# A decoder layer on one core: the triangular inverses of the RWKV part by substitution on VectorE, MoBA heads in pairs, and new orders on four engines

## What is computed

```python
def step(S, inp):                       # RWKV-7, per head (8 heads of 64), over 256 tokens
    r_t, w_t, k_t, v_t, kk_t, a_t = inp
    sa = jnp.einsum('bhvk,bhk->bhv', S, -kk_t)
    S = S * w_t[:, :, None, :] + sa[..., None] * (kk_t * a_t)[:, :, None, :] + v_t[..., None] * k_t[:, :, None, :]
    return S, jnp.einsum('bhvk,bhk->bhv', S, r_t)
...
u = rms_norm(h, norm_mix[l])
z = u @ w_in[l]                         # 1024 x 3328
y_rwkv = rwkv7_time_mix(z[..., :RWKV_IN], ...)
y_moba = moba_attention(q, k, v)        # 8 heads of 64; block 256 = SEQ: plain causal attention here
h = h + jnp.concatenate([y_rwkv, y_moba], axis=-1) @ w_mix_out[l]
h = h + memory_cross_attention(rms_norm(h, norm_xattn[l]), rms_norm(mem, norm_mem[l]), w_xq[l], w_xkv[l], w_xo[l])
a = jnp.square(jax.nn.relu(rms_norm(h, norm_ffn[l]) @ w_ff1[l]))
h = h + a @ w_ff2[l]
out = rms_norm(h, norm_final)
```

## Time and profile before

| | us |
|---|---|
| median of three runs (535.70 to 542.41) | 540.17 |
| the profiled execution, its own time | 539.28 |
| its span, first to last instruction | 537.5 |
| TensorE matmuls busy | 501.6 |
| VectorE busy | 319.7 |
| ScalarE busy | 244.2 |
| GpSimd busy | 34.4 |
| mean granted clock of TensorE | 0.957 |

### The profile page before, as it was taken

How to read it: one execution, slowest core, us unless ns; L and a number is a source line. 1 busy time by engine, 2 the same in 40 slices (tenths; PEclk the granted TensorE clock), 3 DMA queues, 4 the chain that set the end, 5 groups by cost and what they waited for, 6 DMA issues and landing times. The chain is left out here.

```text
span 537.5 us, 13383 instructions
## 1 busy us (share of the span) xinstructions
PE 501.6 (93%) x5926; PEld 464.3 (86%) x5926; DVE 319.7 (59%) x456; ACT 244.2 (45%) x372; POOL 34.4 (6%) x54
## 2 busy tenths in 40 slices
PE   4999999967689799999999999899999999999995
PEld 3999999966568699999999989799899898998984
DVE  4687778874034346467787546837565565655556
ACT  6594763412134242153354436335354453545443
POOL 8200000000000000000430003300000000000000
PEclk9998999997679799999999999989999999999999
DMA  8924547240000033124645323635556555574522
GB/s 256 311 85 154 166 153 233 79 159 5 4 5 4 4 100 111 50 87 149 196 126 172 137 79 95 219 83 195 194 165 224 160 197 195 164 264 157 163 77 78
DMA packets 61421, 73.25 MB, mean 136 GB/s; under 512 B 1314, under 2 KB 51572, under 8 KB 61364
## 3 DMA queue, kind: packets, MB, share of 16 engines
q1 hardware_dynamic: 61284, 72.14, 42.0%
q0 software_dynamic: 80, 0.26, 0.2%
HBM read 71.35 MB, written 1.05 MB: 135 GB/s over the span
## 5 line engine op out<-in xcount | busy, mean ns | idle before, releaser
L1083 ACT ACTIVATE w_hi<-raw 128x1024 fp32r<-128x1024 f32 x130 | 137.2, 1059 | 174.2 <-PE bank L481 110.5
L1593 DVE TENSOR_TENSOR w_lo<-raw,w_hi 128x1024 fp32r<-128x1024 f32 x130 | 160.6, 1240 | 86.9 <-ACT w_hi L1083 86.5
L479 PE MATMUL bank<-op_hi,w_hi 128*128 128x256 f32 x672 | 196.4, 292 | 1.5 <-DVE op_lo L1956 0.7
L480 PE MATMUL bank<-op_lo,w_hi 128*128 128x256 f32 x672 | 192.3, 286 | 0.0
L481 PE MATMUL bank<-op_hi,w_lo 128*128 128x256 f32 x672 | 192.2, 286 | 0.0
L479 PEld LDWEIGHTS bank<-op_hi,w_hi 128*128 128x128 f32 x672 | 131.4, 196 | 3.5 <-DVE op_lo L1956 0.9
L480 PEld LDWEIGHTS bank<-op_lo,w_hi 128*128 128x128 f32 x672 | 131.3, 195 | 0.5
L481 PEld LDWEIGHTS bank<-op_hi,w_lo 128*128 128x128 f32 x672 | 131.1, 195 | 0.0
L496 PE MATMUL bank<-w_hi,op_hi 128*128 128x512 f32 x128 | 50.2, 392 | 0.0
L497 PE MATMUL bank<-w_lo,op_hi 128*128 128x512 f32 x128 | 49.9, 390 | 0.0
L498 PE MATMUL bank<-w_hi,op_lo 128*128 128x512 f32 x128 | 49.8, 389 | 0.0
(11 more groups left out here) (237 smaller groups left out, 590.2 us busy)
## 6 DMA issues: line engine op xcount, KB each, us to landing
raw<-in_w_ff SPq DMA_DIRECT2D x32, 1024.0 KB, 5.3
raw<-in_w_in SPq DMA_DIRECT2D x12, 1024.0 KB, 5.4
raw<-in_w_xkv SPq DMA_DIRECT2D x8, 1024.0 KB, 5.4
raw<-in_w_mix_out SPq DMA_DIRECT2D x4, 1024.0 KB, 4.9
raw<-in_w_xq SPq DMA_DIRECT2D x4, 1024.0 KB, 5.1
raw<-in_w_xo SPq DMA_DIRECT2D x4, 1024.0 KB, 4.9
xval<-in_x SPq DMA_DIRECT2D x2, 512.0 KB, 4.8
raw<-in_w_in SPq DMA_DIRECT2D x2, 512.0 KB, 5.8
```

Source lines behind the costliest of these rows:

```text
L479: mm(dst, wh[:, k, :], op_hi[which][:, k, :], start=first, stop=False)
L480: mm(dst, wh[:, k, :], op_lo[which][:, k, :], start=False, stop=False)
L1083: op(view(w_hi), r, ACT.Copy).then_inc(hi_done, 1)
L1593: tt(view(w_lo), r, view(w_hi).bitcast(f32), ALU.subtract).then_inc(lo_done, 1)
```

## The change

It does four things.

1. The transposed matrices (`nmat`) and the eight products by powers go. VectorE inverts the diagonal blocks of 16 itself (`blocks`): it transposes squares of 32x32 so that each partition holds one block, runs a forward substitution of 14 steps of two instructions over all 128 lanes at once, and transposes back, once straight and once turned.
2. Two products on TensorE (`join`) make the inverse of the whole 32x32 matrix from the diagonal blocks and the corner, and one `solve` applies it. `carry` and `solved` go.
3. MoBA heads run in pairs: the two heads of a pair take the two row halves of the array for the scores and the two column halves for the values, in alternating instructions, and share their ScalarE and VectorE steps where shapes allow.
4. The lists of TensorE, ScalarE and VectorE stand in a new order. `mem` is loaded late; `mats` comes after 42 quarters instead of 55; `residual` and other pieces move; one more quarter stands ahead of `rms(3)`.

```diff
-            def product(b, lhs, rhs):
-                for u in range(NU):
-                    for c in range(4):
-                        last = mm(B[b][chunk(c), CH * u:CH * u + CH], powers[lhs][chunk(c), u, :],
-                                  powers[rhs][chunk(c), u, :], start=True, stop=True)
-                return last
...
+            def join(step):
+                pe.wait_ge(dve_blocks, 1)
...
+                for u in range(NU):
+                    n, h = divmod(u, NH)
+                    corner = X[:, 2 * n + h % 2, 128 * (h // 2):128 * (h // 2) + CH]
+                    for c in range(4):
+                        lhs, rhs = (corner, powers[3][:, u, :]) if step == 0 else (powers[2][:, u, :], powers[4][:, u, :])
+                        last = mm(B[step][chunk(c), CH * u:CH * u + CH], lhs[chunk(c)], rhs[chunk(c)], start=True, stop=True)
+                last.then_inc(pe_join, 1)
...
+            def blocks():
+                dve.wait_ge(dve_mats, 2)
+                dve.wait_ge(dve_side, 1)
+                squares = lambda x: x.rearrange("p u (b t) -> p t b u", b=2)
+                link(nc.vector.transpose(turned.rearrange("p t (b u) -> p t b u", b=2), squares(powers[0])))
+                link(tt(low, turned[:, :, 0:BLK], turned[:, :, BLK:2 * BLK], ALU.add))
+                for t in range(1, BLK - 1):
+                    step = rank_one[:, 0:(BLK - 1 - t) * t].rearrange("p (a j) -> p a j", j=t)
+                    shape = [128, BLK - 1 - t, t]
+                    below = low[:, t + 1:BLK, 0:t]
+                    link(tt(step, low[:, t + 1:BLK, t:t + 1].to_broadcast(shape), low[:, t:t + 1, 0:t].to_broadcast(shape), ALU.mult))
+                    link(tt(below, below, step, ALU.add))
+                link(nc.vector.memset(flat(low)[:, 0:BLK * BLK:BLK + 1], 1.0))
+                for b in range(2):
+                    last = ts(wide[0][:, :, BLK * b:BLK * b + BLK], low.rearrange("p t j -> p j t"), side[:, b:b + 1], None, ALU.mult)
+                link(last)
+                nc.vector.transpose(squares(powers[3]), wide[0].rearrange("p t (b u) -> p t b u", b=2)).then_inc(dve_blocks, 1)
...
+            def pair_scores(i):
...
+                for n, e in ((n, e) for n in range(NT) for e in range(2)):
+                    r, keys = slice(HD * e, HD * e + HD), 128 * (n + 1)
+                    last = mm(B[4 + e][:, 128 * n:128 * n + keys], mqk[r, i, tokens_of(n)], mqk[r, 4 + i, 0:keys],
+                              start=True, stop=True)
...
+            def pair_values(i):
...
+                for e in range(2):
+                    mm(B[5][HD * e:HD * e + HD, 0:256], mval[:, 0, cols(2 * i + e)], probT[:, e, 0:256], start=True, stop=False)
```

More of the change, by code:

```diff
@@ new lines, in values @@
+            def values(h):
+                pe.wait_ge(act_turn, h + 1)
+                pe.wait_ge(dve_scores, min(h + 2, XH))
+                if h:
+                    pe.wait_ge(dve_values, h)
+                pe.wait_ge(out_taken, KIND["xv"][h] + 1)
+                for a in range(2):
+                    for k in range(2):
+                        c = XD * h + 128 * a
+                        last = mm(B[4][:, 256 * a:256 * a + 256], xval[:, k, c:c + 128], xprobT[:, k, :],
+                                  start=(k == 0), stop=(k == 1))
@@ L940, in _ @@
             bonus()
[L941 removed]
+            dense(1)
             mats(0)
             mats(1)
[L944 to L959 removed]
+            spread(1)
@@ L960, in _ @@
+            right(0)
+            right(1)
+            load(1, 0)
+            load(1, 1)
+            dense(1)
             right(2)
-            eighth(1)
+            dense(1)
             right(3)
-            values("m", 2)
-            inverse()
-            turn("m", 3)
-            scores("m", 4)
+            dense(4)
+            join(0)
+            dense(1)
+            join(1)
+            load(1, 2)
+            load(1, 3)
+            dense(6)
+            pair_scores(0)
             solve(0)
@@ L1354, in _ @@
             hi(19)
             hi(20)
-            factor()
             hi(21)
+            tokens()
             hi(22)
+            vtokens()
             hi(23)
+            right(0)
+            load(1, 0)
+            load(1, 1)
+            right(1)
+            right(2)
+            right(3)
             hi(24)
-            scores("m", 0)
             hi(25)
+            join()
             hi(26)
+            load(1, 2)
+            load(1, 3)
             hi(27)
             hi(28)
-            turn("m", 0)
@@ L1385, in _ @@
[L1385 to L1404 removed]
+            hi(31)
@@ L1941, in weigh, with pair_scores @@
-            def weigh(who, h):
-                dve.wait_ge(act_prob, head_no(who, h) + 1)
+            def pair_scores(i):
+                dve.wait_ge(pe_pair, i + 1)
+                if i:
+                    dve.wait_ge(pe_flip, i)
+                for e in range(2):
+                    last = stt(out=prob[:, e, :], in0=B[4 + e][:, 0:384], scalar=HD ** -0.5, in1=causal[:, :],
+                               op0=ALU.mult, op1=ALU.add)
+                link(last)
+                for n in range(NT):
+                    last = nc.vector.reduce_max(small[:, 2 * n:2 * n + 2], prob[:, :, 128 * n:128 * n + 128 * (n + 1)], AX.X, negate=True)
+                last.then_inc(dve_pair, 1)
@@ L2035, in _ @@
             lo(18)
-            keys(1)
+            keys(3)
             take(8)
@@ L2056, in _ @@
             tokens()
-            scores("m", 1)
+            take(9)
+            lo(21)
+            bonus()
+            bonus_bias()
+            lo(22)
+            lo(23)
+            diagonal_of(1)
+            mats(0)
+            spread_copy(1)
+            mats(1)
+            sides()
+            blocks()
+            lo(24)
+            take(10)
+            take(11)
+            lo(25)
+            load(1, 0)
+            load(1, 1)
+            inverse()
+            load(1, 2)
+            load(1, 3)
@@ L2058, in _ @@
+            lo(26)
+            take(12)
             lo(27)
-            weigh("m", 1)
             lo(28)
-            bonus()
             lo(29)
-            bonus_bias()
-            mats(0)
-            mats(1)
-            nmat(0)
-            nmat(1)
-            take(12)
+            pair_scores(0)
+            solve(2)
+            pair_weigh(0)
             take(13)
+            solve(3)
             lo(30)
-            values("m", 0)
-            square()
-            scores("m", 2)
@@ L2154, in _ @@
             operand("mix", 2)
+            take(23)
+            lo(50)
             take(24)
```

870 lines of the change are left out of this document (355 added, 515 removed).

## The result

The changed kernel took 501.8 us in the median of four executions (505.9, 497.7, 496.3 and one of 1568.8 us, whose cause is not known), the kernel before 538.3 us beside it. The forecast was 503: close to the median, and some 7 us above these three. But for the one of 1568.8, executions of the changed kernel lie further apart than those of before (494 to 507 us against 536 to 542), and the first profile was taken of a long one, 505.9 us; a second one, taken later of the same kernel, is of a short one, 496.1 us.

The account below looks back on a forecast made before the run. TensorE was taken as the bound, its middle stretch as the place to gain. 539.3 - 17.7 - 17.2 - 3.0 - 4 - 1.6 - 1.4 - 2 + 2 + 2 + 6 = 502.4, predicted as 503 us, range 489 to 516.

Parts of the forecast that it names:

- Small matmuls and stops: TensorE's middle stretch: 1,152 small records removed, -17.7 us; fewer stops at blocks of 256 instructions, -17.2 us.
- 30.4 us of stops before: Middle stretch, kernel before: sixteen blocks with 32.0 us of work wait 16 x 3.9 - 32.0 = 30.4 us.
- floor of 3.9 us per block: A block of 256 TensorE instructions takes at least about 3.9 us; seven short blocks then wait 13.2 us after.
- the cut into single blocks: TensorE's instruction list of each kernel, cut into blocks of 256 with each record's own pace, to count the stops.
- Would-show list: Signs if right: 38 packets, stops only around `mats`, joins, `outq`, 3.5 to 4.3 us apart, `gate` near 211 us.
- Blocks on VectorE: `blocks` ahead of the first join: 10.6 us in all, 11.4 to be covered by 14.6 on TensorE, so 0.
- waits of +2 behind it: +1 us for splits and takes waiting behind `blocks`, +1 for `outq`, whose last copy stands behind a weigh.
- +2 of the early stretch: Up to about 78 us: VectorE prepares the earlier `mats` at nine tenths busy; +2 us of waits, most at `keys`.
- Pairs: MoBA heads run two together in different array halves: -4 us, between 0 and -6.6.
- Start: First dense quarter runs ahead of the parameters, whose DMA cost 1.63 us: -1.6 us.
- `rms(3)`: One more quarter ahead of `rms(3)`, where TensorE waited 2.45 us for GpSimd: -1.4 us.
- +6 for two dips: Dense quarters behind `mats` and `outq` run at halved clock, two dips of 3.0 us each: +6 us.

Follow-up runs that it names:

- burst: The changed kernel plus 368 unused small products in one piece, ten dense quarters behind `rms(3)`: 524.6 us, ratio 0.965 to the kernel before.
- same_half: The changed kernel with both heads of a MoBA pair on the same half of the array: 510.6 us, ratio 0.947 to the kernel before.
- spread: The changed kernel plus 368 unused small products, eight behind each of 46 dense quarters after `rms(3)`: 523.0 us, ratio 0.970 to the kernel before.
- chunks: The changed kernel plus 368 unused small products in eight pieces of 46, five dense quarters between pieces: 508.7 us, ratio 0.946 to the kernel before.
- late_blocks_2: The changed kernel with eight more chained copies of 512 elements inside `blocks` on VectorE: 501.3 us, ratio 0.931 to the kernel before.

## Why the prediction was right, step by step

**Small matmuls and stops.** The mechanism held: 128 matmuls per stop, no semaphore, 38 packets, and -12 us when six products are taken from the kernel before. The sizes were less good. The 30.4 us of stops before are not idle time that the trace shows: from `mats` to `phi` TensorE was idle for 16.9 us, in nine stops and not sixteen, and the other 16.5 us stand in its busy time (60.8 less 44.3 of own work), at a mean clock of 0.78. The size of what remains was taken as 13.2 us from a floor of 3.9 us per block, read in a stretch where the DMA engines stood idle (0.08). There the period was right: 3.5 to 3.7 us in `burst`. In the new places weights are being loaded, and from stop to stop it was 5.9 us (89.52 to 95.44) and 6.0 (115.61 to 121.63). Against that, the cut into single blocks had a stop at every crossing, and `burst` ran 247 records before its first one, so it passed one crossing without a stop. The errors have opposite signs: 8.5 us in the short execution, 15.7 in the long one. Behind `gate`, where dense work is long, the view of waits has no stop without a semaphore in either profile of the changed kernel (from 206.93 and 216.90 to the end); among small matmuls and just behind them (L443) it has, and 368 small ones in one piece cost about 12 us more than in eight, the clock included (20.5 less 8.7).

**Would-show list.** "Each ending 3.5 to 4.3 us after the last one" failed for the reason just given. "Only around `mats`, the joins and `outq`" failed by the stop at L443, which begins 1.5 us behind the joins. The idle time ahead of `rms(3)` was 0.45 us where about 1.0 was forecast. `gate` at 206.9 or 216.9 lies on either side of 211.

**Blocks on VectorE.** Its timeline (of the first profile):

```profile
99.43 1.06 DVE L1740 STREAM_TRANSPOSE neu<-neu 128x512 f32<-128x512 f32 x1
...
100.98 0.17 DVE L1746 TENSOR_TENSOR neu<-neu 128x14 f32<-128x14 f32 x1
...
108.59 1.13 DVE L1752 STREAM_TRANSPOSE neu<-neu 128x512 f32<-128x512 f32 x1
```

The 28 steps, the first of them shown, last from 100.98 to 107.6, 6.6 us where 6.4 were estimated. The three transposes are 1.06, 1.13 and 1.17 us and not 0.69: the whole is 11.9 us, not 10.6. The cover held as worked out, since even twice 0.69 left room; the first join at 111.61 comes 1.9 us behind the signal. So this term stayed 0, and the waits of +2 behind it came to 0.3 (L442 above). The +2 of the early stretch are about right: 0.6 us at 18.6, 0.8 at 65.9, 0.2 at `keys`.

**Pairs.** -4 was too small: -6.6, the bound, is what the rows show (8 records in 0.86 and 0.80 us, where one head took 0.85 and 0.8), and `same_half` takes 5.1 of it away. A pair takes what one head took before (0.86 against 0.85 us for the scores); on the same half it takes 1.50.

**Start.** -1.6 for the earlier first quarter was wrong: 0. The step that failed is that the forecast priced the removed wait at the front and didn't ask what the later row sums make late behind it. The forecast nowhere had the slow pace of the start (dense matmuls 0.21 us apart in the kernel before from 12.15 to 16.0, though the granted clock is 1.00 there), which ended at 12.5 and 13.3 us instead of 17 in the two profiles of the changed kernel, and early with the old order of the start too (its first dense matmuls 0.12 us apart stand at 13.91).

**`rms(3)`.** -1.4 was too small: the wait is 2.0 us shorter, and the forecast left out the halved clock behind it. At 0.21 us instead of 0.12, the 23 dense matmuls from 349.5 to 354.2 had cost 2.2 us more. In all 3.8 us are saved behind `gate`.

**Clock.** The forecast's 0.12 and 0.21 us per dense matmul, and with them its quarter of 1.44, are the pace of the earlier trace rows: 20.30 to 20.42 at a granted clock of 1.00 (20.2 to 22.0), and 0.21 to 0.22 at 0.50 (45.08 to 45.30, 349.51 to 349.72). +6 for two dips was too much for the dense matmuls, and it left out the small ones. From `mats` to `gate`, 17 dense matmuls of the short execution and 45 of the long one started 0.21 us apart at the half clock (0.50), which is 1.6 and 4.2 us at 0.094 us each. (As many again, 18 and 17, are the first of a dense group at the full clock (1.00); their successor comes 0.20 to 0.22 later, too.) But small matmuls run slower as well: in the short execution a right side behind the stop of the `mats` took 1.63 us at a granted clock of 0.50 (91.68 to 93.31), and one at 1.00 took 0.78 (97.01 to 97.79).

**The sum again.** With these terms (stops, pairs, `rms(3)` with the clock behind it, start, waits, clock) put at what the short execution shows, the sum gives about 488 and not 496.1; with those of the long one about 498 and not 505.9. Both times some 8 us are missing, so the 503 owes part of its closeness to errors of opposite signs. Two things that the sum doesn't have go some way: small matmuls at the half clock (0.85 us for the one right side above), and the changes between dense and small work. From `mats` to `gate` there are 20 dense groups behind small ones, where there were 13, and at 0.26 us for each change there and back the seven are 1.8 us. That is argued from `spread`, not shown, and the rest is open.

## What to carry to other kernels

Count TensorE's instructions, not only its time: where 128 small matmul records with their loads held less than about 4 us of work here, and up to 6 while large transfers ran, the engine stood still with no semaphore in the trace, and with five dense quarters between pieces of 46 no stop was left among them (`chunks`). Put small matmuls in groups of some dozens: here each group cost 0.26 us for the change from dense work and back (`spread`), and in one piece they stopped for 1.5 to 4.7 us at each of four blocks (`burst`). Look at the clock behind a wait, and not only at the wait: at `rms(3)` it cost as much again. When a wait is removed at the front of a chain, follow what the moved work makes late before booking the gain.

## What the runs showed of the hardware that was not expected

- Blocks of 256 TensorE instructions arrive 3.5 to 3.7 us apart when they are wanted back to back (`burst`), and 5.9 to 6.1 us apart in the long execution while 1 MB loads of weights run; the packets then move at the end of such a load, 87.0, 93.1 and 119.2 us against ends at 87.3, 93.4 and 119.7. In the kernel before it is the same (packets at 112.9 and 117.1, ends at 113.1 and 117.6), though 4.2 us apart, with loads that end 4.5 us apart, where those of the long execution end 6.1 apart (87.3 and 93.4).
- One program has executions in which such a packet comes about 1.5 us ahead of a load of weights and others in which it comes 3.5 us after the load's start. In the `mats` the two profiled ones differ by 5 us of stops, and by 9.8 us in all (496.1 and 505.9). Why the packet is late isn't shown.
- A change from dense matmuls (float32r, whole array) to 32x32 ones in float32 and back costs 0.26 us beyond the work; 0.18 of it are lost at a float32 group on the whole array too.
- Two heads in different row or column halves take the time of one (0.86 us for the scores, where one head took 0.85, and 0.80 for the values, where it took 0.8) even when the second head's matmuls are issued behind all of the first's.
- VectorE's transpose of 512 float32 elements per partition takes 1.06 to 1.17 us, where an instruction with two inputs of that size took 0.69 and a copy 0.43 (`late_blocks_2`).
